# Blocks 2 and 3: last four output tiles and first four gate/up tiles by token halves, with a norm for each half

## What is computed

```
h = h + gate * (attention @ w_out)                 # "out2", "out3"
f = rms_norm(h, g) * (1 + scale) + shift           # "ffn0", "ffn1"
u = f @ w_up                                       # "gu2", "gu3"
y = conv_b + sum over j of shifted(u) * conv_w[j]  # causal, over three tokens
h = h + gate * (silu(y_gate) * y_val) @ w_down     # "down2", "down3"
```

## Time and profile before

| | us |
|---|---|
| median of 3 runs | 1979.87 |
| lowest, highest | 1978.61, 1982.14 |
| span of the profiled execution | 1976.5 |
| TensorE busy in it | 1930.4 (98%) |
| GpSimd busy | 1247.1 (63%) |
| VectorE busy | 1085.3 (55%) |
| ScalarE busy | 563.2 (28%) |

### The profile page before, as it was taken

How to read it: one execution, slowest core, us unless ns; L and a number is a source line. 1 busy time by engine, 2 the same in 40 slices (tenths; PEclk the granted TensorE clock), 3 DMA queues, 4 the chain that set the end, 5 groups by cost and what they waited for, 6 DMA issues and landing times.

```text
span 1976.5 us, 26794 instructions
## 1 busy us (share of the span) xinstructions
PE 1930.4 (98%) x9306; PEld 1555.4 (79%) x9306; DVE 1085.3 (55%) x1656; ACT 563.2 (28%) x1119; POOL 1247.1 (63%) x729
## 2 busy tenths in 40 slices
PE   9999999999999899999999999999989999999999
PEld 7867788888888787777788888877766778888887
DVE  5956589787787424464443442243988543434412
ACT  4135300001125335662311121132457431211210
POOL 7641688887666566555766666645775357666664
PEclk9999999999999899999999999999999999999999
DMA  7520277676542121114233333313220023333231
GB/s 276 207 81 12 84 267 256 233 249 208 195 156 80 60 96 48 59 43 149 86 96 97 96 99 95 99 50 103 77 73 1 19 64 115 99 98 96 96 96 64
DMA packets 62327, 221.17 MB, mean 112 GB/s; under 512 B 6907, under 2 KB 7163, under 8 KB 62124
## 3 DMA queue, kind: packets, MB, share of 16 engines
q1 hardware_dynamic: 45216, 161.71, 25.8%
q10 hardware_dynamic: 17036, 58.46, 8.1%
HBM read 218.00 MB, written 2.14 MB: 111 GB/s over the span
## 4 chain that ended last, share of the span: by engine, by line
PE 93%; DVE 2%; POOL 2%; issue 2%; ACT 1%; DMA 0%; SPq 0%; POOLq 0%; DVEq 0%; ACTq 0%
PE bank L310 26%; PE bank L312 25%; PE bank L311 25%; PE bank L940 2%; PE bank L773 2%; PE bank L345 1%; PE bank L350 1%; PE bank L346 1%; PE bank L457 1%; PE bank L899 1%; PE bank L950 1%; PE bank L795 1%; POOL w_lo L1284 1%; PE bank L464 1%; PE bank L596 1%
## 5 line engine op out<-in xcount | busy, mean ns | idle before, releaser
L1284 POOL TENSOR_TENSOR w_lo<-raw,w_hi 128x1024 fp32r<-128x1024 f32 (+1 forms) x304 | 764.9, 2517 | 24.8
L310 PE MATMUL bank<-a_hi,w_hi 128*128 128x512 f32 x1960 | 764.8, 390 | 0.4 <-issue 0.3
L312 PE MATMUL bank<-a_hi,w_lo 128*128 128x512 f32 x1960 | 762.8, 389 | 0.0
L311 PE MATMUL bank<-a_lo,w_hi 128*128 128x512 f32 x1960 | 762.7, 389 | 0.0
L1279 POOL TENSOR_SCALAR w_hi<-raw 128x1024 fp32r<-128x1024 f32 x298 | 346.0, 1161 | 472.4 <-PE bank L312 357.9
L310 PEld LDWEIGHTS bank<-a_hi,w_hi 128*128 128x128 f32 x1960 | 367.9, 188 | 77.7 <-POOL w_lo L1284 0.9
L312 PEld LDWEIGHTS bank<-a_hi,w_lo 128*128 128x128 f32 x1960 | 367.9, 188 | 76.9
L311 PEld LDWEIGHTS bank<-a_lo,w_hi 128*128 128x128 f32 x1960 | 368.0, 188 | 75.8
L1882 DVE SCALAR_TENSOR_TENSOR tmp<-bank,vecs,tmp 128x511 f32<-128x511 f32 x88 | 65.9, 749 | 259.6 <-ACT tmp L1572 259.6
L1867 DVE CUSTOM_DVE_ANT_0 y<-y,cond 128x1024 f32<-128x1024 f32 x84 | 195.4, 2360 | 0.0
L1572 ACT ACTIVATE tmp<-bank,vecs 128x512 f32<-128x512 f32 x88 | 68.5, 781 | 372.3 <-PE bank L312 364.6
(11 more groups left out here) (292 smaller groups left out, 2268.7 us busy)
## 6 DMA issues: line engine op xcount, KB each, us to landing
raw<-in_stream SPq DMA_DIRECT2D x299, 512.0 KB, 3.5
y<-in_ada ACTq DMA_DIRECT2D x96, 512.0 KB, 4.4
x<-in_x SPq DMA_DIRECT2D x4, 512.0 KB, 7.0
bias<-in_bias ACTq DMA_DIRECT2D x1, 2048.0 KB, 13.4
y<-rel_rows ACTq DMA_DIRECT2D x1, 2048.0 KB, 8.3
bias<-rel_rows ACTq DMA_DIRECT2D x1, 2048.0 KB, 16.0
out<-x SPq DMA_DIRECT2D x8, 256.0 KB, 2.0
cond<-in_c ACTq DMA_DIRECT2D x1, 512.0 KB, 6.5
```

The lines of the kernel that those rows point to most:

```text
L310: pe.matmul(o, lhs_hi, rhs_hi, start=start, stop=False, **kw)
L311: pe.matmul(o, lhs_hi, rhs_lo, start=False, stop=False, **kw)
L312: return pe.matmul(o, lhs_lo, rhs_hi, start=False, stop=stop, **kw)
L1284: m = pool.tensor_tensor(w_lo[:, s, part], raw[:, j, part], f32(w_hi[:, s, part]), ALU.subtract)
```

## The change

Token halves: h = 0 is tokens 0 to 255, h = 1 tokens 256 to 511.

- **Output tiles 4 to 7** are worked for h = 0 first, all four (into banks 0 and 1, two half tiles in one bank), then for h = 1 (banks 2 and 3). Each is 24 matmuls with 256 columns. The weights' slots are held until the second half, since only that counts up `block_done`.
- **The norm** is made for each half: its own adding of `x`, squares, adding of squares (`piece`: tiles 0 to 3 whole, then 4 halves for h = 0, 4 for h = 1), sum, inverse and spread. The sum of h = 0 stands on TensorE after tile 4's second half, its spread after tile 5's. The sum of h = 1 stands after chunk 3 of the first pair of gu2, its spread at that pair's end.
- **Gate/up tiles 0 to 3** are worked in the order pair (0, 1) for h = 0, pair (2, 3) for h = 0, pair (0, 1) for h = 1, pair (2, 3) for h = 1.
- **All `a_lo`** of these two norms are made by VectorE; GpSimd has none of them and only splits weights.
- The four `ffn0`, `ffn1` uses change in both blocks alike. Counters that these steps move are renumbered.

```
+        def pe_sum_half(pe, name, h):
+            pe.wait_ge(sq_added, ADDED_AT[name] + (7, HALF_PIECES - 1)[h])
+            for t in (2 * h, 2 * h + 1):
+                m = pe.matmul(sum_columns(name)[:, t:t + 1], square_sum[...], ones[:, 0:1], ...)
+            m.then_inc(group_used, 1)
+
+        def pe_spread_half(pe, name, h):
+            pe.wait_ge(inverse_step, 5 * (inverse_index(name) + h) + 5)
+            if h:
+                pe.wait_ge(scaled_ready, T_AT[name] + DC)
+            for t in (2 * h, 2 * h + 1):
+                m = pe.transpose(rstd_bank[:, t * P:(t + 1) * P], rms[:, 1, t:t + 1].broadcast_to([P, P]), ident)
+            m.then_inc(rstd_ready, 1)
+
+        def pe_late_halves(pe, name, norm):
+            for h in range(2):
+                for c in range(4, DC):
+                    s = (START[name] + c) % SPLIT
+                    if h == 0:
+                        pe.wait_ge(split_ready, START[name] + 1 + c)
+                    if c % 2 == 0:
+                        pe.wait_ge(x_ready, X_AT[name] + 2 * h + (c - 4) // 2 + 1)
+                    for k in range(DC):
+                        m = pe_three_passes(pe, late_tile(c, h), ..., a_hi[:, k, tokens_of(h)], a_lo[:, k, tokens_of(h)], ...)
+                    m.then_inc(block_done if h else half_done, 1)
+                    if h and c == 4:
+                        pe_sum_half(pe, norm, 0)
+                    if h and c == 5:
+                        pe_spread_half(pe, norm, 0)
+
+        def pe_early_halves(pe, name, norm, update):
+            pe_begin(pe, name)
+            pe.wait_ge(x_ready, X_AT[update] + 8)
+            for h in range(2):
+                for pair in range(2):
...
+                    for k in range(DC):
+                        if pair == 0:
+                            pe.wait_ge(hi_ready, SPLIT_AT[norm] + DC * h + k + 1)
+                        for o, s in tiles:
...
+                        if pair == 0:
+                            pe.wait_ge(lo_ready, LOW_AT[norm] + DC * h + k + 1)
+                        for o, s in tiles:
...
+                        if h == pair == 0 and k == 3:
+                            pe_sum_half(pe, norm, 1)
+                    if h == pair == 0:
+                        pe_spread_half(pe, norm, 1)
```

On VectorE (`add_piece` is the adding of a square, `late_tiles` the adding of two half tiles to `x`, `scale`, `low` as before but of 256 tokens):

```
-            dve_residual(v, "out2", 0, 2, ..., 4, "ffn0")
-            dve_diag(v, "ffn0", add=False)
-            dve_scale_split(v, "ffn0", "ffn0", DC, ...)
+            dve_halved_norm(v, "out2", 0, 2, "ffn0", ...)
...
+            late_tiles(6, 0)
+            add_piece(6)
+            add_piece(7)
+            inverse(0)
+            late_tiles(4, 1)
+            v.wait_ge(rstd_ready, NORM_INDEX[name] + 1)
+            for c in range(DC):
+                scale(0, c)
+                if c:
+                    low(0, c - 1)
+                if c in (1, 2):
+                    add_piece(7 + c)
+                if c == 4:
+                    late_tiles(6, 1)
+                if c in (5, 6):
+                    add_piece(5 + c)
+            low(0, DC - 1)
+            inverse(1)
+            v.wait_ge(rstd_ready, NORM_INDEX[name] + 2)
+            for c in range(DC):
+                scale(1, c)
...
```

On ScalarE and GpSimd:

```
-            act_x_squares(a, "ffn0", "out2")
-            act_rms(a, "ffn0")
-            act_high(a, "ffn0", DC, shift=lambda c: mod(0, 3, c))
+            act_halved_norm(a, "out2", "ffn0", lambda c: mod(0, 3, c))
...
-            split_stream(START["out2"] + SPLIT + 2, START["gu2"] + AHEAD)
-            pool_lows("ffn0")
-            split_stream(START["gu2"] + AHEAD, START["qi"] + AHEAD)
+            split_stream(START["out2"] + SPLIT + 2, START["qi"] + AHEAD)
...
-            pe_tiles(pe, "out2", "battn", norm="ffn0")
-            pe_norm(pe, "ffn0", 1)
-            pe_tiles(pe, "gu2", "ffn0")
+            pe_tiles(pe, "out2", "battn", end=4)
+            pe_late_halves(pe, "out2", "ffn0")
+            pe_early_halves(pe, "gu2", "ffn0", "out2")
+            pe_tiles(pe, "gu2", done=4)
```

More of the change, by code:

```diff
@@ L354, in pe_tile_pair, with tokens_of, piece, late_tile @@
                     after(k)
-        def pe_tiles(pe, name, split=None, norm=None):
-            n = COUNT[name]
+        def tokens_of(h):
+            return slice(HALF * h, HALF * h + HALF)
+        def piece(p):
+            if p < 4:
+                return p, slice(0, S)
+            return 4 + p % 4, tokens_of(p // 4 - 1)
+        def late_tile(c, h):
+            return bank[2 * h + (c - 4) // 2][:, HALF * (c % 2):HALF * (c % 2) + HALF]
+        def pe_sum_half(pe, name, h):
+            pe.wait_ge(sq_added, ADDED_AT[name] + (7, HALF_PIECES - 1)[h])
+            for t in (2 * h, 2 * h + 1):
+                m = pe.matmul(sum_columns(name)[:, t:t + 1], square_sum[:, GROUP_AT[name] % 2, t * P:(t + 1) * P], ones[:, 0:1],
+                              start=t == 0, stop=True, skip_group_check=True)
+            m.then_inc(group_used, 1)
@@ L360, in pe_tiles @@
+        def pe_tiles(pe, name, split=None, norm=None, done=0, end=None):
+            n = COUNT[name] if end is None else end
             follows = {"u": "z", "q": "u"}.get(name)
-            if not follows and name not in ("ki", "pe_gate"):
+            if not follows and name not in ("ki", "pe_gate") and not done:
                 pe_begin(pe, name)
-            done = 0
             if split == "attn":
@@ L1536, in _ @@
                          lambda c: low_done("dattn", c), ready=((q_placed, 14), (q_placed_late, 2)))
-            pe_tiles(pe, "out3", "dattn", norm="ffn1")
-            pe_norm(pe, "ffn1", 1)
-            pe_tiles(pe, "gu3", "ffn1")
+            pe_tiles(pe, "out3", "dattn", end=4)
+            pe_late_halves(pe, "out3", "ffn1")
+            pe_early_halves(pe, "gu3", "ffn1", "out3")
+            pe_tiles(pe, "gu3", done=4)
             pe_down(pe, "down3", 2)
@@ L2117, in _ @@
             dve_stick(v)
[L2118 to L2120 removed]
+            dve_halved_norm(v, "out2", 0, 2, "ffn0", lambda c: gains[:, 1, c:c + 1], lambda c: mod(0, 3, c))
             dve_conv(v, 0)
             dve_split_hidden(v, "down2")
[L2123 removed]
+            dve_residual(v, "down2", 0, 5, lambda c: wait_down(v, 1, c), "mix1")
             dve_diag(v, "mix1", add=False)
```

153 lines of the change are left out of this document (117 added, 36 removed).

## The result

The changed kernel takes 1985.26 us (median of 14 runs, 1983.32 to 1987.86) against 1980.43 us for the kernel before beside it (14 runs): a ratio of 1.0024, 95% interval 1.0017 to 1.0031. The forecast was 1981 with a range of 1970 to 1986. The range holds the time, but the change costs 4.8 us and not 1.3, just past the 0.2% that I called no change: the result is rival 3's time. The time lies within 1 us of the upper end, so it was the width of the range that held it and not the sum. The next rows say why.

The account below looks back on a forecast made before the run. TensorE bounds the kernel. A first seam of 57.6 us plus 6.9 of waits gives 64.5, winning 0.9 over both seams; 2.2 of clock loss makes it 1.3 slower, near 1981 us, range 1970 to 1986.

Parts of the forecast that it names:

- rival 3: Both seams: the low clock outlasts the stall, a seam loses 3.0 us instead of 1.1, near 1985 us; chance 0.12.
- What bounds the kernel: TensorE, busy 98% of the span, bounds the end; 10.7 and 10.4 us could be won in the two seams.
- The contention: First token half: GpSimd's splits hold up VectorE operations reading two SBUF tensors; 6.9 us a seam returns as TensorE waits.
- a sign: In the changed trace TensorE waits 1 to 3 us each time for VectorE, 6 to 7 us a seam.
- Rival 1: Seams: contention is missed and halves work as drawn; seam 58.4 us, about 1967 us in all; chance 0.10.
- Sums and spreads: TensorE in each seam: two sums of about 0.5 us and two spreads of 0.3 us, 1.6 us together.
- The pace: Half tiles in each seam: 384 matmuls of 256 columns at 0.1175 us each, 1.6 us more a seam.
- The clock: End of each seam's stall: the clock falls and dense work runs at 1.2 GHz, losing 0 to 1.8 us, taken as 1.1.
- Rivals 2 and 4: Seams: two VectorE operations per GpSimd boundary, near 1973 us, chance 0.12; or 256-column pace 0.120 us, about 1983, no chance given.
- Rival 4: Half tiles: 256-column matmuls take 0.120 us instead of 0.1175, 1.0 us more a seam, about 1983 us; no chance given.
- Covers at nothing: Seams: ScalarE's extra square roots, renumbered counters, the raw-block stream and VectorE's eight more lows in h = 1 cost nothing.

Follow-up runs that it names:

- filled waits: Changed kernel with 8, 38 and 31 small matmuls that nothing reads ahead of TensorE's three waits: 1980.78 us, ratio 1.0001 to the kernel before.
- scaled chunks in PSUM: Changed kernel with only the scaled chunks in PSUM, so lows read one SBUF operand and sums of squares still two: 1977.57 us, ratio 0.9983 to before.
- before, idle time filled: Kernel before with 21, 17 and 26 small matmuls that nothing reads ahead of TensorE's three waits in the seam: 1978.33 us, ratio 0.9987.

## Why the prediction was right, and which step was off

**What bounds the kernel: right.** The end moved by what TensorE lost in the two seams, 5.3 us in the traces, 4.8 in the timed runs.

**The contention: right, mechanism, place and size.** It was read from one addition and one low of the seam and two lows at the start of the program. Five slow operations in a row, one at each boundary of GpSimd's operations, came as drawn: 936.5, 937.7, 940.3, 941.4 and 943.9 for the forecast 934.7, 935.9, 938.4, 939.6 and 942.2, all 1.7 to 1.9 later, as the whole seam began 1.2 later and ran at the slower pace. TensorE waits 0.81, 2.70 and 2.17 us for the forecast 1.1, 3.0 and 2.7. These 5.7 us are short of the 6 to 7 that I gave as a sign; they undersell it, since the low clock stretches the matmuls ahead of the third wait. At a full clock the contention costs 65.15 - 58.82 = 6.33 us, against 64.5 - 58.4 = 6.1 between my sum and my rival without it. One row that I read for it didn't bear on it: the scales of 941.86 ran while GpSimd stood idle; that scales aren't held up is seen only in the changed kernel. The two experiments that take away one side of the contention each show that it is the cause.

**What would be left without it: right.** Rival 1 gave a seam of 58.4 and 1967 us. Both kernels without contention are at 58.8 and 1968: the mechanism of the sum holds for this case too, and what spoke against it, that GpSimd's four blocks have no other time, is what happened.

**Sums and spreads: right.** 58.82 - 54.41 - 0.32 leaves 4.1 us for pace and these, 1.5 of it beside the pace's 2.6. The sum had 1.6. No run prices them apart.

**The pace: too low.** I took 0.1175 us for a matmul of 256 columns, between half of a whole one and the rows. The rows said 0.12, and 0.120 it is, in the changed kernel and, by 1.23 us for 96 matmuls, with nothing else changed. That is 2.6 us a seam where I had 1.6, or 2.0 over both, more than the whole 1.3 of the forecast. The error was to settle between a measured value and an argument.

**The clock: the term that failed.** I took 1.1 us a seam, a little above the middle of 0 to 1.8, for "the fall may come at any point of the stall". The upper end was set by the low stretch before. The experiment with filled waits prices the clock at 3.1 and 1.8 us in the first trace, 2.0 and 2.5 in the second, 4.5 us over both seams in the timed runs, not 2.2. What was wrong was the upper end. Before, the waits of a seam lay close together with only the sum and the spread between them, the low level began among them, and 3.6 and 4.3 us of it met dense work. Here more work stands between the three waits, and the fall comes within the second or up to 1 us behind it (944.5 in seam 1), so that 4 to 7 us of low level lie behind the last wait over dense work. That is rival 3 ("the three waits are spread, so the fall may come late"), whose fall at 945 came at 944.5; its low stretch of 7 us was 10.2 there. I had the reason for it in hand, gave it 12%, and kept the milder size in the sum. With 0.120 and rival 3's 3.0 the sum would have been 54.4 + 2.6 + 1.6 + 6.9 + 3.0 = 68.5, and 68.24 was measured in seam 1; in seam 2, at a clock loss of 1.8, 67.3 for 66.87. Rival 3's 5.2 us over both seams are near the measured 5.3 in part by luck: it had the pace 2.0 too low and the clock, at 6.0, above its 4.9.

**Rivals 2 and 4.** Two of VectorE's operations at one boundary came in no trace: one each among the five of the changed kernel, and one each where only the lows or only the squares were left. Rival 4 happened, and was set aside as "no case of its own" though it and the clock push the same way: each was small against 4 us, both together were not.

**Covers at nothing: right.** No wait for weights at tile 4 (split by 969.8, begun at 971.81), none in the second half, and none of TensorE's for a square root.

## What to carry to other kernels

Before you move VectorE work to a place beside GpSimd, list which of its operations read two SBUF tensors; price each at the rest of a GpSimd operation, and put one operand in PSUM if a bank is free: here that was worth 17 us of 1985 and turned a loss of 0.24% into a gain of 0.63%. When a gap is replaced by several short waits, price the low clock also for the case that it begins late in them and lies over the dense work behind, and add up the small terms that point the same way before calling them no case of their own. A stretch that must wait anyway can be filled with matmuls that nothing reads; see first what is next to be late, since in the kernel before most of the gain went to a wait for weights.

## What the runs showed of the hardware

- A VectorE operation with two SBUF operands doesn't run beside one of GpSimd's that reads SBUF: with one operand in PSUM the same low takes 0.48 us under the same GpSimd work, not 2.24. One gets in at each boundary of GpSimd's and ends 0.27 to 0.29 us behind it, at 256 columns, in all five traces with such operations. GpSimd pays as well: 1.22 us for a TENSOR_SCALAR of 1.05.
- Once the clock was at its low level, it stayed there into dense work for several us, and how far differs between seams and executions of one kernel: in the changed one, 7 and 4 us behind the last wait in one trace, 4.5 and 5.5 in the other. It fell behind idle times of 1.50 and 1.28 us with little work between (before) and behind a single one of 2.67 (scaled chunks in PSUM); it stayed up through a single wait of 1.33 us (before, idle time filled).
- A 256-column matmul of this kind takes 0.120 us and one of 512 0.2267: halving costs 0.006 to 0.007 us per half matmul, 2.6 us for the 384 of a seam here.
